# Two-layer diffusion step on one Trainium2 core: expert rows by one-hot product, expert outputs added by DMA, and a ring of 16 weight homes

## The reference, cut to what matters

```python
for l in range(DEPTH):                       # 2 layers
    h = rms_norm(x, norm1_g[l]) * (1 + sc1) + sh1
    x = x + ga1 * mixer(h)                   # layer 0: conv and spatial gate; layer 1: Fourier and attention
    h = rms_norm(x, norm2_g[l]) * (1 + sc2) + sh2
    x = x + ga2 * hier_moe(h, ...)
y = rms_norm(x, final_norm_g)

def hier_moe(h, wg, bg, we, be, w1, w3, w2):
    ...                                      # one group by argmax, in it the top 2 of 4 experts
    hid = silu(h @ w1[e]) * (h @ w3[e])      # 1024 -> 256, each of 16 experts
    return sum over e of (hid * gates[e]) @ w2[e]     # 256 -> 1024
```

## Time and profile before

| | us |
|---|---|
| median of 3 runs | 806.44 |
| lowest and highest | 806.28, 810.97 |
| the profiled execution | 812.16 |
| its span in the profile | 810.3 |
| PE busy in that span | 707.8 |
| mean granted PE clock | 0.942 of full |

### The profile page before, as it was taken

One profiled execution on the slowest core, in us unless ns is written; L12 is line 12 of the kernel. 1 busy time (PEld: TensorE's weight loads), 2 busy tenths in 40 slices (PEclk: granted clock), 3 DMA queues, 4 the chain that ended last, 5 costly groups with the idle time before them and its releaser, 6 DMA issues.

```text
span 810.3 us, 9735 instructions
## 1 busy us (share of the span) xinstructions
PE 707.8 (87%) x3677; PEld 397.1 (49%) x3678; DVE 233.7 (29%) x485; ACT 140.5 (17%) x288; POOL 177.6 (22%) x232
## 2 busy tenths in 40 slices
PE   2788999999989997899989898798799899999940
PEld 0334444554555654466344553455445556666620
DVE  1200212222162232122340423355221722322315
ACT  2201000001211121121130211345111121221201
POOL 4000111110421222122130100465314122222203
PEclk9899999999988999899999999899799889999975
DMA  9999798493074999988684512904200859979934
GB/s 340 391 344 354 294 361 334 182 407 140 26 296 136 420 422 420 420 347 338 250 351 169 214 47 99 421 7 153 101 33 27 311 187 416 377 273 420 420 146 170
DMA packets 52620, 213.97 MB, mean 264 GB/s; under 512 B 13985, under 2 KB 21153, under 8 KB 33393
## 3 DMA queue, kind: packets, MB, share of 16 engines
q1 hardware_dynamic: 31520, 178.59, 55.3%
q0 software_dynamic: 10240, 24.38, 8.4%
q10 hardware_dynamic: 10832, 10.63, 4.1%
HBM read 207.57 MB, written 15.43 MB: 275 GB/s over the span
## 4 chain that ended last, share of the span: by engine, by line
PE 68%; DMA 18%; DVE 6%; issue 3%; ACT 2%; POOL 1%; SPq 1%; ACTq 0%; POOLq 0%; DVEq 0%
PE ps L1304 14%; PE ps L1235 11%; PE ps L1329 7%; DMA pool<-in_mod_w 7%; PE ps L1378 7%; DMA pool<-in_moe_w 6%; PE ps L1422 5%; PE ps L1172 4%; PE ps L1539 3%; PE ps L1395 3%; PE ps L1467 2%; PE ps L1288 2%; DMA pool<-y_rows 2%; PE ps L1225 2%; PE ps L1521 1%
## 5 line engine op out<-in xcount | busy, mean ns | idle before, releaser
L1304 PE MATMUL ps<-pool 128*64 128x256 f32 x1280 | 146.9, 388 | 8.7 <-issue 6.7
L1304 PEld LDWEIGHTS ps<-pool 128*64 128x64 f32 x1280 | 106.6, 140 | 53.6 <-issue 21.3
L1235 PE MATMUL ps<-pool,yT 128*128 128x512 f32 x192 | 86.5, 606 | 0.0
L1329 PE MATMUL ps<-pool 128*64 128x512 f32 x320 | 73.1, 597 | 4.6 <-DMA pool<-in_moe_w 2.1
L1172 PE MATMUL ps<-pool,cs 128*32 128x512 f32 x384 | 49.3, 645 | 24.0 <-DMA pool<-in_mod_w 13.7
L1378 PE MATMUL ps<-hT,pool 128*128 128x384 f32 x192 | 65.6, 496 | 0.0
L1235 PEld LDWEIGHTS ps<-pool,yT 128*128 128x128 f32 x192 | 36.4, 194 | 42.4 <-issue 42.2
L534 POOL TENSOR_SCALAR pool<-pool 128x384 f32<-128x384 f32 (+1 forms) x36 | 36.5, 1029 | 77.2 <-DVE pool L1102 77.1
L1378 PEld LDWEIGHTS ps<-hT,pool 128*128 128x128 f32 x192 | 37.2, 198 | 31.5 <-issue 10.3
L932 DVE SCALAR_TENSOR_TENSOR pool<-ps,pool 128x256 f32<-128x256 f32 x20 | 9.7, 484 | 128.8 <-PE ps L1304 128.8
L1329 PEld LDWEIGHTS ps<-pool 128*64 128x64 f32 x320 | 25.0, 136 | 38.9 <-issue 37.4
(11 more groups left out here) (220 smaller groups left out, 785.5 us busy)
## 6 DMA issues: line engine op xcount, KB each, us to landing
pool<-in_moe_w SPq DMA_DIRECT2D x96, 1024.0 KB, 13.3
pool<-in_mod_w SPq DMA_DIRECT2D x24, 2048.0 KB, 11.1
pool<-in_ev_w_in SPq DMA_DIRECT2D x6, 1024.0 KB, 20.6
pool<-in_ev_w_in SPq DMA_DIRECT2D x2, 2048.0 KB, 24.3
ga<-mods POOLq DMA_DIRECT2D x8, 512.0 KB, 6.8
pool<-in_ev_w_out SPq DMA_DIRECT2D x2, 2048.0 KB, 10.6
pool<-mods POOLq DMA_DIRECT2D x8, 512.0 KB, 8.7
pool<-in_od_w_out SPq DMA_DIRECT2D x2, 2048.0 KB, 10.1
```

Of the source, the lines that this page charges most:

```text
L1235: ins = mm(ps[:, 2 * t + n, :], yT[:, k, t * P:(t + 1) * P], weight(parts[k // 4], 4, D)[:, k % 4, n * 512:n * 512 + 512], start=k == 0, s ...
L1304: ins = mm(ps[m, k, 0:DE], hTe.rearrange("p (c n) -> p c n", c=DC)[:, cc, m], w[e][:, cc, :], start=cc == 0, stop=cc == DC - 1)
L1329: ins = mm(ps[m, 4 + n, :], hidT[:, cc, m], w2[e][:, cc, n * 512:n * 512 + 512], start=cc == 0, stop=cc == 1)
```

## The change

It has four parts. (1) The first step's rows of each layer are no longer gathered: PE makes them, already turned, as the product of `xn` with a one-hot matrix `first_hot` (`first_rows`). (2) The last step's rows are no longer scattered: its output stays in `hg`, and PE sums it into token order by a one-hot product (`last_rows`, into PSUM banks 0 to 5). All other rows are added to `x` by six DMAs of POOL's queue that accumulate in their destination; they start when all scatters but the last step's have landed. For this there is one `y_rows` for each layer, both set to zero early on by eight DMAs of ACT's queue. (3) The ring has 16 homes of 1 MB, used in eight pairs: two experts' same matrix go to one pair of homes. The four new ones are in `hT`, `yT` and two thirds of `xn`. PE's and SP's loops over pairs are written out. (4) Parts 1 to 3 of the `mod1.1` product, and `put_mods(1, 1)` with what follows it, come later; part 0 stands before `last_rows`; the nine fillers and those of `step_contents` are gone, and `first_rows` has three.

```diff
-UNROLL = 2
-TURNS = PAIRS // UNROLL
+RING_PAIRS = 8
+KINDS = ("gate_mm", "up_mm", "down_mm")
...
+        nothing = scratch(4608, 1536)
+        first_hot = scratch(3072, T).rearrange("p (t n) -> p t n", t=TILES)
...
+            for s in order:
+                used = {}
+                for o in (owner[s], owner[s + 1]) if s < NSLOT else ((("router_mm", 3 * (l + 1)), ("h_rows", 16 * TILES * (l + 1)), (f"L{l}_x_tr", 1))[0:s - NSLOT + 1]):
...
-        places = [expert_places(0, (6, 7, 10, 11, 8, 9, 4, 5, 0, 1, 2, 3))]
+        places = [expert_places(0, (6, 10, 8, 4, 0, 2, 12, 14))]
...
-        places.append(expert_places(1, (0, 1, 2, 3, 10, 4, 5, 11, 6, 7, 8, 9)))
+        places.append(expert_places(1, (2, 6, 8, 10, 4, 0, 12, 14)))
...  SP
+                    else:
+                        before, kind = divmod(n - RING_PAIRS, 3)
+                        wait_used((KINDS[kind], l), step_entry(before))
...
-                if n == split + 4:
+                if n == split + 6:
                     sp.wait_ge(S("y_rows2"), 32)
...  POOL
-                gather_start(l, of_rows[:, 0:1])
-                gps.wait_ge(S(f"L{l}_x_tr"), 1)
                 gather_start(l, of_rows[:, 1:2])
...
-                scatter_start(l)
+                gps.wait_ge(S("rows_landed"), l + 1)
+                for k in range(2):
+                    for t in range(TILES):
+                        if k:
+                            gps.wait_ge(S(f"y_rows{t}"), 32 * l + 16)
+                        gps.dma_start(x[:, t, :], y_rows[l][k * T + t * P:k * T + (t + 1) * P, :], accum_op=ALU.add) \
+                            .then_inc(S(f"y_rows{t}"), 16)
...
-            put_mods(1, 1)
             for t in range(TILES):
                 root("norm", 2 * TILES + t + 1, t, D)
-            take_columns(1, 1, (1,))
-            gps.wait_ge(S("x2"), TILES)
-            take_gate(1, 0)
             for t in range(TILES):
                 root("qc", t + 1, t, QL)
                 root("kvc", t + 1, 3 + t, KVL)
+            put_mods(1, 1)
...  ACT
-                act.wait_ge(S(f"L{l}_stored"), n * 16)
-                act.wait_ge(S(f"L{l}_hTe"), n * 2 + 2)
-                for t in range(TILES):
-                    for k in range(2):
-                        act.dma_start(yg[k][:, t * D:(t + 1) * D], y_rows[k * T + t * P:k * T + (t + 1) * P, :]) \
...
+                act.wait_ge(S(f"L{l}_stored"), but_last * 16)
+                act.sem_inc(S("rows_landed"), 1)
...
+            act.wait_ge(S("nothing"), 1)
+            for l in range(2):
+                for part in range(4):
+                    act.dma_start(y_rows[l].rearrange("(p r) d -> p (r d)", p=P)[:, 1536 * part:1536 * (part + 1)], nothing).then_inc(S("zeroed"), 16)
...  DVE, project_out
+                dve.wait_ge(S("zeroed"), 128)
...  DVE, place_tokens
+                link(v_.scalar_tensor_tensor(R["half"], R["step"], FAR, R["place"], ALU.mult, ALU.add))
+                dve.wait_ge(S("h_made"), 2 * (l + 1))
+                for t in range(TILES):
+                    ins = v_.tensor_scalar(first_hot[:, t, :], iota, R["half"][:, t, 0:1], None, ALU.is_equal)
+                link(ins)
+                for t in range(TILES):
+                    ins = v_.scalar_tensor_tensor(first_hot[:, t, :], iota, R["half"][:, t, 1:2], first_hot[:, t, :], ALU.is_equal, ALU.add)
+                ins.then_inc(S("first_hot"), 1)
...  DVE, experts (after the loop, for the last step)
+                for t in range(TILES):
+                    ins = v_.tensor_scalar(last_hot[:, t, :], cst[:, C_IOTA:C_IOTA + P], last_at[:, t:t + 1], None, ALU.is_equal)
+                dve.wait_ge(S(f"L{l}_down_mm"), n)
+                rows_done(hg)
...
-                    link(v_.tensor_tensor(x[:, t, :], x[:, t, :], a, ALU.add))
-                    v_.tensor_tensor(x[:, t, :], x[:, t, :], b, ALU.add).then_inc(S("x2"), 1)
+                    dve.wait_ge(S("combined"), TILES * l + t + 1)
+                    v_.tensor_tensor(x[:, t, :], x[:, t, :], bank2(2 * t, D), ALU.add).then_inc(S("x2"), 1)
...  DVE (mod_rows(1, 1) moved from ahead of experts_out(0) to behind the copies of z)
-            mod_rows(1, 1)
...  PE
-                keep_clock(3, 1)
+                keep_clock(2, 1)
...
+            def first_rows(l):
+                keep_clock(3, 1)
+                pe.wait_ge(S("h_made"), 2 * (l + 1))
+                pe.wait_ge(S("h_last"), l + 1)
+                pe.wait_ge(S("first_hot"), l + 1)
+                for cc in range(DC):
+                    for t in range(TILES):
+                        ins = mm(bank2(2, D)[:, cc * P:(cc + 1) * P], xn[:, t, cc::DC], first_hot[:, t, :],
+                                 start=t == 0, stop=t == TILES - 1)
+                ins.then_inc(S(f"L{l}_x_tr"), 1)
+            def last_rows(l, n):
+                pe.wait_ge(S(f"L{l}_ys"), n + 1)
+                pe.wait_ge(S(f"L{l}_hTe"), n * 2 + 2)
+                for t in range(TILES):
+                    for half in range(2):
+                        ins = mm(ps[:, 2 * t + half, :], last_hot[:, t, :], hg[:, half * 512:(half + 1) * 512], start=True, stop=True)
+                    ins.then_inc(S("combined"), 1)
...
-                    keep_clock((4, 0)[v], 1)
...
-                keep_clock(2, 1)
-                pe.wait_ge(S(f"L{l}_gathered"), 16)
-                turn_rows(range(DC))
...
+                if l == 0:
+                    mod_part(1, 1, 0)
+                last_rows(l, n)
...
-            for part in range(4):
-                mod_part(1, 1, part)
-            keep_clock(9, 6)
+            mod_part(1, 1, 1)
             norm_transposes(1)
...  (after the products of z)
+            for part in (2, 3):
+                mod_part(1, 1, part)
```

More of the change, by code:

```diff
@@ L104, in program @@
         mods = nc.dram_tensor("mods", (2, 2, 6 * D), F32, kind="Internal").ap()
-        y_rows = nc.dram_tensor("y_rows", (2 * T, D), F32, kind="Internal").ap()
+        y_rows = [nc.dram_tensor(f"y_rows{l}", (2 * T, D), F32, kind="Internal").ap() for l in range(2)]
         h_rows = nc.dram_tensor("h_rows", (T, D), F32, kind="Internal").ap()
@@ new lines, in experts @@
+                for n in range(3 * PAIRS):
+                    pair, k = divmod(n, 3)
+                    if n < RING_PAIRS:
+                        for key, v in waits[n].items():
+                            if waited.get(key, 0) < v:
+                                wait_used(key, v)
+                                waited[key] = v
+                    else:
+                        before, kind = divmod(n - RING_PAIRS, 3)
+                        wait_used((KINDS[kind], l), step_entry(before))
+                    s0 = order[n % RING_PAIRS]
+                    for e in range(2):
+                        sp.dma_start(expert_slot(s0 + e), (moe_w1, moe_w3, moe_w2)[k][l, 2 * pair + e:2 * pair + e + 1]
+                                     .rearrange("a (p c) n -> p (a c n)", p=P)).then_inc(S(f"slot{s0}"), 16)
@@ L1027, in _ @@
                 v_.tensor_copy(z[:, t, 0:512], ps[:, 2 * t, :]).then_inc(S("z_low"), 1)
+            mod_rows(1, 1)
             for t in range(TILES):
@@ L1280, in experts @@
             def experts(l):
-                before = places[l][1]
                 halves = [slice(e * HALF, (e + 1) * HALF) for e in range(2)]
@@ L1290, in turn_rows, with pair_arrived, up @@
                             ins.then_inc(S(f"L{l}_x_tr"), 1)
-                def slots(u, k):
-                    return [3 * (2 * u + e) + k for e in range(2)]
-                def slots_arrived(u, k, i):
-                    for s in slots(u, k):
-                        pe.wait_ge(S(f"slot{s}"), i * 16 + 16 * (before[s] + 1))
-                def up(u, k, chunks):
-                    w = [pool[:, s * SLOT:(s + 1) * SLOT].rearrange("p (c n) -> p c n", c=DC) for s in slots(u, k)]
+                def pair_arrived(pair, k):
+                    s, value = expert_pair(l, pair, k)
+                    pe.wait_ge(S(f"slot{s}"), value)
+                def up(pair, k, chunks):
+                    w = [expert_slot(expert_pair(l, pair, k)[0] + e).rearrange("p (c n) -> p c n", c=DC) for e in range(2)]
                     for cc in chunks:
@@ L1321, in step @@
                     turn_rows(range(4, DC))
-                    slots_arrived(u, 2, i)
-                    w2 = [pool[:, s * SLOT:(s + 1) * SLOT].rearrange("p (c n) -> p c n", c=2) for s in slots(u, 2)]
+                    pair_arrived(pair, 2)
+                    w2 = [expert_slot(expert_pair(l, pair, 2)[0] + e).rearrange("p (c n) -> p c n", c=2) for e in range(2)]
                     pe.wait_ge(S(f"L{l}_hidT"), j + 1)
```

168 lines of the change are left out of this document (85 added, 83 removed).

## The result

The changed kernel takes 819.97 us (median of 4 runs, 819.5 to 825.91); the kernel before took 807.95 us in the same set (4 runs, 806.28 to 810.97). The ratio is 1.016, with a 95% interval of 1.010 to 1.022. So it is slower by 12 us, where 17.5 us less were forecast, and outside the range. The profiled execution took 820.32 us, with a span of 818.4 against 810.3.

A forecast was written before the change was run, and what follows sets the result against it. PE, busy 707.8 of 810.3 us, and its waits were taken as the bound. Ring -13.7, lead-ins 0, layer 0's end and behind it -2.8 - 0.8 + 1.0 + 2.8, layer 1's end -4.0: -17.5, so 789 us, range 773 to 800.

The forecast's parts named there:

- The ring: Layer 0's expert stage: 16 homes load weights earlier, PE never waits; -13.7 us, bounds 14 and 8.
- Rival (c): Layer 0's expert stage still starves in part, losing 6 of the 13.7 us: 795 us; chance 0.12 together with (e), late homes.
- The lead-in: Before each layer's first gate product: one-hot products replace the gather, small gain eaten by clock; 0, ends -1.7 and +9 us.
- Rival (b): Clock falls in both lead-ins and at `z`: main sum plus 9.1 and 2.4, 800 us; chance 0.12.
- Zeroing: Ahead of `project_out`: eight writes, 15 us of DMA work, delay DVE's adds but 11 us are covered; nothing, up to +3.
- The end of a stage: Last down product to whole `x`: adding DMAs end last, `x` whole 15.3 us behind; -2.8 us layer 0, -4.0 layer 1.
- The price of 2.5 us for an adding DMA: Stage ends: each accumulating DMA takes twice 1.25 us because the bytes read are doubled; bounds 1.25 and 3.5 us.
- (a): Stage ends: adding DMAs run like plain reads, sum -31.6, 775 us; chance 0.18.
- (d): Stage ends: accumulating DMAs make it slower than before, even at 3.95 us each, 831 us at 6 each; chance 0.11.
- the earlier load: Layer 0, whole `x` to `z`: `od_w_in` issued before the last down product ends, so `z` waits less; -0.8 us.
- Behind `z`: Between `z` and the Fourier product: moved `mod1.1` parts and DVE's row work no longer free; +2.8 us, between +1.5 and +4.
- The start of `z` at half clock: Layer 0: PE idle without fillers before `z`, so it starts at half clock; +1 us, 0 to 3.4.

The follow-up runs named there:

- the fastest kernel: Kernel before with 16-home ring, gather, `last_rows`, plain reads for adding DMAs, and `od_w_in` loads held until `y_rows` is read back: 788.13 us, ratio 0.978.
- the gather alone: Changed kernel with only part (1) undone: first step's rows gathered again, with the fillers of before; 804.67 us, ratio 0.999 against the kernel before.

## Why the prediction was wrong

**The ring: -13.7 forecast.** The stage fell by 10.1 us in the changed kernel and by 13.0 where its first step ran at full clock, so the mechanism was right and the size nearly so. But the forecast put the stall on a median that moves by 11 us with the clock. Alone, the ring shows as -0.4%, with an interval from -0.9% to nothing, and why most of its 10.7 us is missing there stays open. Rival (c), that a part of the waiting stays, came true to some 2 us where the stage starts early (126.6 to 127.1 us in the three kernels with ring and gather whose first gate product starts near 251), and hardly in the changed kernel, with its one wait of 0.76 us.

**The lead-in: 0 forecast, with ends at -1.7 and +9; +7.8 and +8.9 measured, and 2.9 and 2.7 more in the first steps.** This is the step that failed. "PE then does 24 products of 128x128 by 128 columns. Three of them took 0.67 us at full clock, so 24 take 5.4" takes its price from products whose weights lie side by side; these lie 32 bytes apart and cost 11.66 us. In layer 0 the forecast had 6.3 us from the ranking to these products, 5.4 for them and 4.8 behind them; the trace has 7.5, 11.5 and 6.2. So 6.1 of the 8.8 us that were missed there are this one term. The code said so (`xn[:, t, cc::DC]`), and the trace of before held a price of stepped weights. First its ordinary 64-column loads, then those of `mrow[0][:, 0, cc::DC]` (line 1182), which have the same step, grouped by line (busy, mean ns):

```profile
L1304 PEld LDWEIGHTS ps<-pool 128*64 128x64 f32 x1280 | 106.6, 140 | 53.6 <-issue 21.3 <-DVE pool L926 2.2 <-DMA pool<-in_moe_w 1.0
...
L1182 PEld LDWEIGHTS ps<-cst,mrow 128*64 128x64 f32 x32 | 2.0, 216 | 1.8 <-DVE mrow L737 1.8
```

216 against 140 ns for the same tile, and the stepped ones stand in a stretch granted 0.97 to 1.00. Twice that excess for 128 columns, on 48 loads, would have been 7.3 us, an estimate; 6.1 came. But the same trace has the loads of the turns, 128 columns at the same step, at 193 ns, and who had taken these for the nearest row would have seen nothing. The Trainium skill ("SBUF — State Buffer", Door 1: The DMA port swizzle) says that SBUF is read in lines of 16 bytes and that fp32 data can be stepped by up to 4 elements for free. Here the step is 8, so it gives the direction, and the two traces agree with it (192 and 335 ns). It gives no price, and that is what the rows have.

The clock was seen as the danger but put at the wrong place. It did not fall under `first_rows`, which ran at 1.00, but behind it: in the second of the two small products (2.75 us instead of 1.51), and in most of the first step, at 2.9 us for layer 0. Rival (b), with 0.12, had the clock fall in both lead-ins. It did fall in both layers, but the 9.1 us of that rival were for `first_rows` itself, and the two first steps, which no term named, cost 5.6.

**Zeroing: nothing.** DVE waited for it, PE didn't: in the changed kernel's timeline DVE's first add of `project_out` comes 6.8 us later than in the earlier trace rows, and the products of `project_out` begin and end within 0.4 us of before.

```profile
193.03 0.69 DVE L802 TENSOR_TENSOR xn<-ps,ga 128x512 f32<-128x512 f32 x1 [14.03 <-DMA y_rows<-pool]
```

**The end of a stage: -2.8 and -4.0 forecast; +5.3 and -0.9 measured.** The price of 2.5 us for an adding DMA was right, so rivals (a) and (d) fall. The reason given, twice the bytes to read, fits DMA engines that were full at 207 GB/s, but no run shows those bytes, and no row stood behind the factor of two: there was luck in it. Two other terms were wrong. The start: forecast 2 us ahead of the last down product's end, in fact 1.0 us behind it in layer 0,

```profile
387.65 2.81 POOL L449 DMA_DIRECT2D x<-y_rows  x3 [9.61 <-ACTq L630]
```

because the last scatter landed after 10.30 us, beside the loads of `od_w_in` that the change lets out earlier. The forecast took ACT's last copy as the latest event, and not that landing; and it counted the earlier load as a gain. In layer 1, without such loads, the start was 2.6 us ahead, yet the forecast 16.0 us for six became 19.8 from the first issue to the last landing: 5.65 us until the first had landed (2.1 more than 2.5 + 1), and 3.9 between the waves (1.4 more).

**Behind `z`: +2.8 forecast, +2.7 measured** (10.4 - 7.7). The start of `z` at half clock: the turns took 5.04 us, 0.7 more than at full clock in the fastest kernel (4.34); +1 forecast.

By profile, then: -17.5 + 3.6 (ring, of which 2.9 is the clock) + 16.7 (lead-ins) + 1.9 (stage of layer 1, where the first step alone lost 2.7) + 8.1 + 3.1 (ends) + 0.1 (whole `x` to `z`) - 0.1 (behind `z`) gives +15.9. The span grew by 8.1. What stands between are the stretch up to the ranking and that from behind `z` to the ranking of layer 1 (-2.1 and -5.7), where single executions differ (the second profile of before has 2.0 and 6.7 less there than the first, without any change). The median's +12 lies between the two.

## What to carry to other kernels

Look at how an operand lies before taking a price from a row of the same shape: a product whose weights are picked with a step costs by its weight load, and a gather that looked clumsy was cheaper than it. When work that was overlapped with fillers is replaced by short dependent products, look at the clock of what comes behind it too, and not only under it. When a bulk load is moved ahead in a queue, write down which small transfer on the critical path now shares the DMA engines with it; here one wait moved from behind the scatter to behind the reads was worth 9 us.

## What the runs showed of the hardware

- A load of 128 fp32 weights took 192 ns when they lay side by side and 335 ns at a step of 32 bytes, with 24 products at 5.60 and 11.66 us. The stepped one was as long in a stretch granted 0.61 as in one granted 0.98. The loads of the turns, at the same step, took 193 ns, and 143 side by side.
- POOL's DMAs that add 512 KB from DRAM into SBUF landed 2.5 to 2.7 us apart within a wave of three, with the DMA engines full at 207 GB/s; plain reads of the same size kept them full at 397 GB/s, and six had landed some 10 us behind their first issue.
- A scatter of one step's rows (at most 128 of 4 KB) landed after 10.30 us beside 3.7 MB of weight reads, and after 7.8 us without them, with a DMA share of 0.52 to 0.55 from other transfers.
- Granted clock: 0.50 for some 10 us behind a lead-in with PE gaps of 1.05 and 1.19 us between small products, and 1.00 at the same place with two fillers in the gaps. With the gather and the fillers of before it was 1.00 there in the profiles of before and 0.50 in that of the gather alone.
